# ScalarE scales the neighbouring tokens, VectorE joins them in one operation, and the key norms lie with tokens on partitions

## What is computed

```python
z = h @ w_in[l]
u_a, g_a = z[..., :D_POOL], z[..., D_POOL:2 * D_POOL]
sh = z[..., 2 * D_POOL:2 * D_POOL + D_SHIFT]          # 13 tiles of 128 channels
sh_prev = jnp.pad(sh, ((0, 0), (1, 0), (0, 0)))[:, :-1]
sh = sh + shift_mu[l] * (sh_prev - sh)                # the token shift
...
kk = heads(k * k_k)                                   # 8 heads of 64 channels
kk = kk / jnp.maximum(jnp.sqrt(jnp.sum(kk * kk, axis=-1, keepdims=True)), 1e-12)
k = k * (1.0 + (a - 1.0) * k_a)
```

## Time and profile before

| | |
|---|---|
| median of 3 runs | 1616.11 us (1614.89 to 1616.32) |
| profiled execution | 1613.78 us, its span 1612.0 us |
| TensorE busy in the span | 1548.9 us (96%) |
| VectorE, ScalarE, GpSimd busy | 788.5 (49%), 619.6 (38%), 525.0 us (33%) |
| the stage of the change | 1267 to 1408.6 us |
| VectorE busy, 1270 to 1310 us | 39.4 of 40 us |
| TensorE busy, 1300 to 1310 us | 3.2 of 10 us |
| GpSimd's weight subtraction L469 | 2425 ns in the mean |

### The profile page before, as it was taken

The page is one execution under the profiler, slowest core; times in us unless marked ns, Lnnn a source line. Parts: engine busy times, 40 slices in busy tenths (PEclk is TensorE's granted clock), DMA queues, the critical chain, the costliest instruction groups (busy, mean ns, idle before and its releaser), DMA issues.

```text
span 1612.0 us, 31406 instructions
## 1 busy us (share of the span) xinstructions
PE 1548.9 (96%) x12704; PEld 1381.6 (86%) x12704; DVE 788.5 (49%) x1374; ACT 619.6 (38%) x1139; POOL 525.0 (33%) x233
## 2 busy tenths in 40 slices
PE   8999998999999999999999999999999989999996
PEld 7898887999999999999989888888889867777765
DVE  5444443754132231575446642322316898656656
ACT  5666664443232231442224532322224534433322
POOL 2222222044444444124440444444441244450010
PEclk9999999999999999999999999999999999999998
DMA  5111111222222222223222222232222222200001
GB/s 200 53 54 53 56 64 52 67 93 92 93 94 92 93 93 92 76 80 105 91 91 80 91 93 92 93 103 92 91 92 79 66 92 78 92 16 3 3 27 52
DMA packets 35691, 125.69 MB, mean 78 GB/s; under 512 B 4080, under 2 KB 4336, under 8 KB 35568
## 3 DMA queue, kind: packets, MB, share of 16 engines
q1 hardware_dynamic: 35568, 123.90, 23.8%
HBM read 121.79 MB, written 2.10 MB: 77 GB/s over the span
## 4 chain that ended last, share of the span: by engine, by line
PE 71%; DVE 10%; issue 2%; ACT 2%; POOL 0%; DMA 0%; DVEq 0%; POOLq 0%; ACTq 0%; SPq 0%
PE G L1493 59%; PE G L1823 3%; PE ST L1823 3%; PE PO L1823 2%; PE PV L1823 2%; DVE wlo L931 1%; DVE t L1233 1%; DVE m L951 1%; PE ST L1459 1%; PE ST L1493 1%; DVE hres L958 1%; DVE acc L1383 0%; DVE z L1236 0%; POOL wlo L469 0%; DVE rstd L892 0%
## 5 line engine op out<-in xcount | busy, mean ns | idle before, releaser
L469 POOL TENSOR_TENSOR wlo<-raw,whi 128x1024 fp32r<-128x1024 f32 x207 | 501.7, 2425 | 1050.5 <-ACT whi L521 738.6
L1493 PE MATMUL G<-xh,whi 128*128 128x258 f32 (+3 forms) x1504 | 367.1, 307 | 9.4 <-DVE wlo L931 4.1
L1493 PE MATMUL G<-xl,whi 128*128 128x258 f32 (+3 forms) x1504 | 357.5, 300 | 0.0
L1493 PE MATMUL G<-xh,wlo 128*128 128x258 f32 (+3 forms) x1504 | 355.9, 299 | 1.1 <-DVE xl L899 1.1
L1493 PE MATMUL G<-ah,whi 128*128 128x256 f32 (+2 forms) x1024 | 278.3, 313 | 1.9 <-DVE al L1118 1.6
L1493 PE MATMUL G<-ah,wlo 128*128 128x256 f32 (+2 forms) x1024 | 276.6, 311 | 0.0
L1493 PE MATMUL G<-al,whi 128*128 128x256 f32 (+2 forms) x1024 | 276.5, 311 | 0.0
L1493 PEld LDWEIGHTS G<-xh,whi 128*128 128x128 f32 x1504 | 242.6, 189 | 32.9 <-issue 10.8
L1493 PEld LDWEIGHTS G<-xh,wlo 128*128 128x128 f32 x1504 | 243.9, 189 | 10.8 <-DVE xl L899 1.3
L1493 PEld LDWEIGHTS G<-xl,whi 128*128 128x128 f32 x1504 | 243.0, 189 | 9.8
L531 ACT ACTIVATE whi<-raw 128x1024 fp32r<-128x1024 f32 x96 | 101.9, 1061 | 388.3 <-PE G L1493 388.3
(11 more groups left out here) (332 smaller groups left out, 1988.1 us busy)
## 6 DMA issues: line engine op xcount, KB each, us to landing
raw<-weights_dram SPq DMA_DIRECT2D x225, 512.0 KB, 3.5
hres<-xT_dram SPq DMA_DIRECT2D x8, 264.0 KB, 4.7
out_dram<-hres SPq DMA_DIRECT2D x8, 256.0 KB, 2.1
con<-consts_dram SPq DMA_DIRECT2D x1, 512.0 KB, 7.2
mat<-mats_dram SPq DMA_DIRECT2D x1, 512.0 KB, 8.0
con<-consts_dram SPq DMA_DIRECT2D x1, 264.0 KB, 6.4
vec<-vecs_dram SPq DMA_DIRECT2D x1, 171.0 KB, 6.1
con<-consts_dram SPq DMA_DIRECT2D x1, 128.0 KB, 4.0
```

The lines of the kernel that those rows point to most:

```text
L469: nc.gpsimd.tensor_tensor(wlo[:, s], raw[:, s % 2], whi[:, s].bitcast(F32), ALU.subtract)\
L1493: last_of[0] = nc.tensor.matmul(to[:, p0:p1], wt[:, w, ws], xt[:, k, t0 - off:t1_ - off], start=k == 0 and q == 0, stop=k == KT - 1 and q ...
```

## The change

Token shift: instead of the difference and the product on VectorE, ScalarE multiplies the neighbouring tokens with mu into `t1`, and VectorE joins tile x (1 - mu) + `t1` in one operation; 1 - mu is made once for all 13 tiles (`keep`, 128x13) behind the zeroing of the pads. ScalarE's scaling of tile i stands in its loop at j = i + 1, ahead of the weight split of that step, and ahead of the whole loop ScalarE waits for `pads_set`.

Key norms: `blk` becomes the moving operand with two of its columns, and the squares the stationary one, four times 128 tokens. The result is 128x8: tokens on partitions, and for each of four token groups the two heads of the pair. Root, maximum and reciprocal work on 128x8 (`kin`). To bring the result back to channels on partitions, TensorE multiplies for each token group and head a column of `kin`, repeated 64 times as weights, with the identity: eight products of 128 moving columns onto 64 output rows in bank 6, from which L1276 (now L1282) reads. For pair 0 this stands behind block 6, for the others behind the block of step i = 3. The sum of the next pair waits until bank 6 has been read (`kk_ready`) where it waited for the root (`kn_ready`).

```diff
--- before.py
+++ after.py
@@ -218,6 +218,8 @@
         BK = sb("BK", [P, PAIRS, NCH, 2, CH], F32, second)
         bonus = sb("bonus", [P, PAIRS, SEQ], F32, second)
         g_end = sb("g_end", [P, PAIRS, NCH], F32, second)
+        keep = sb("keep", [P, 13], F32, second)
+        kin = sb("kin", [P, 8], F32, second)
         Sg = sb("Sg", [P, CH], F32, second)
         ET, B8 = (b.rearrange("p (c t) -> p c t", t=CH) for b in (k2[:], z[:, 0, 1:]))
         second.close()
@@ -781,7 +783,15 @@
             mlp(1, OUT, 3, (2, 0))
 
 
+            act.wait_ge(S("pads_set"), 4)
             for j in range(25):
+                if 1 <= j <= 13:
+                    i = j - 1
+                    act.wait_ge(tile_out, B_IN2 + j)
+                    if i >= 2:
+                        act.wait_ge(S("shifted"), i - 1)
+                    nc.scalar.activation(t1[:, i % 2, PAD:], z[:, Z_SLOT[i], 0:SEQ], ACT.Copy, scale=col(V_MU, Z_SLOT[i]))\
+                        .then_inc(S("shift_step"), 1)
                 split(B_IN2 + j + HELD, (B_IN2 + j) % 4)
                 p, i = feature_step(j)
                 if j == 1:
@@ -800,7 +810,7 @@
                 if i == 1:
 
                     act.wait_ge(S("knorm_sum"), p + 1)
-                    nc.scalar.activation(kn[:], bank(6), ACT.Sqrt).then_inc(S("kn_ready"), 1)
+                    nc.scalar.activation(kin[:], bank(6)[:, 0:8], ACT.Sqrt).then_inc(S("kn_ready"), 1)
                     act.wait_ge(S("cp_ready"), p + 1)
                     nc.scalar.activation(Gt[:], cs[:], ACT.Exp, scale=-DECAY).then_inc(S("Gt_ready"), 1)
                     nc.scalar.activation(Gi[:], cs[:], ACT.Exp, scale=DECAY).then_inc(S("Gi_ready"), 1)
@@ -1208,7 +1218,8 @@
             nc.vector.memset(z[:, :, 0:1], 0.0).then_inc(S("pads_set"), 1)
             nc.vector.memset(zu[:, :, 0:PAD], 0.0).then_inc(S("pads_set"), 1)
             nc.vector.memset(t1[:, :, 0:PAD], 0.0).then_inc(S("pads_set"), 1)
-            dve.wait_ge(S("pads_set"), 3)
+            nc.vector.tensor_scalar(keep[:], vec[:, V_MU:V_MU + 13], -1.0, 1.0, ALU.mult, ALU.add).then_inc(S("pads_set"), 1)
+            dve.wait_ge(S("pads_set"), 4)
             def input_tile(j):
 
                 b = B_IN2 + j
@@ -1227,14 +1238,9 @@
 
                     i = j - 1
                     zi = z[:, Z_SLOT[i]]
-                    dve.wait_ge(tile_out, b)
-                    if i >= 2:
-                        dve.wait_ge(S("shifted"), i - 1)
-                    nc.vector.tensor_tensor(t1[:, i % 2, PAD:], zi[:, 0:SEQ], zi[:, 1:], ALU.subtract)\
-                        .then_inc(S("shift_step"), 1)
                     dve.wait_ge(S("shift_step"), i + 1)
-                    nc.vector.scalar_tensor_tensor(zi[:, 1:], t1[:, i % 2, PAD:], col(V_MU, Z_SLOT[i]), zi[:, 1:], ALU.mult,
-                                                   ALU.add).then_inc(S("shifted"), 1)
+                    nc.vector.scalar_tensor_tensor(zi[:, 1:], zi[:, 1:], keep[:, Z_SLOT[i]:Z_SLOT[i] + 1], t1[:, i % 2, PAD:],
+                                                   ALU.mult, ALU.add).then_inc(S("shifted"), 1)
                 p, i = feature_step(j)
                 if i == 0 and p or j == 2 + 5 * PAIRS:
 
@@ -1262,9 +1268,9 @@
                 elif i == 2:
 
                     dve.wait_ge(S("kn_ready"), p + 1)
-                    nc.vector.tensor_scalar(kn[:], kn[:], 1e-12, None, ALU.max).then_inc(S("km_ready"), 1)
+                    nc.vector.tensor_scalar(kin[:], kin[:], 1e-12, None, ALU.max).then_inc(S("km_ready"), 1)
                     dve.wait_ge(S("km_ready"), p + 1)
-                    nc.vector.reciprocal(kn[:], kn[:]).then_inc(S("kr_ready"), 1)
+                    nc.vector.reciprocal(kin[:], kin[:]).then_inc(S("kr_ready"), 1)
                 elif i == 3:
 
                     dve.wait_ge(S("Gp_ready"), p + 1)
@@ -1272,8 +1278,8 @@
                     dve.wait_ge(S("shifted"), 3 * p + 3)
                     nc.vector.scalar_tensor_tensor(sg[:], zr, col(V_RK, p), k2[:], ALU.mult, ALU.mult)\
                         .then_inc(S("rk_ready"), 1)
-                    dve.wait_ge(S("kr_ready"), p + 1)
-                    nc.vector.scalar_tensor_tensor(cs[:], zk, col(V_KK, p), kn[:], ALU.mult, ALU.mult)\
+                    dve.wait_ge(S("kn_spread"), p + 1)
+                    nc.vector.scalar_tensor_tensor(cs[:], zk, col(V_KK, p), bank(6), ALU.mult, ALU.mult)\
                         .then_inc(S("kk_ready"), 1)
                     nc.vector.tensor_tensor(zr, zr, Gt[:], ALU.mult).then_inc(S("R_ready"), 1)
                     dve.wait_ge(S("kk_ready"), p + 1)
@@ -1832,6 +1838,13 @@
                     some(bank(ahead % 4), ahead % 4, range(KT), x2h, x2l, META, [(*OUT, 0, SEQ)])
                     last_of[0].then_inc(block_done, 1)
                 p, i = feature_step(j)
+                if j == 6 or i == 3 and p:
+                    pe.wait_ge(S("kr_ready"), p + 1)
+                    for t in range(4):
+                        for x in range(2):
+                            last = mm(bank(6)[ROW[x], P * t:P * t + P],
+                                      kin[:, 2 * t + x:2 * t + x + 1].to_broadcast([P, HD]), ident)
+                    last.then_inc(S("kn_spread"), 1)
                 if i == 0 and p or j == 2 + 5 * PAIRS:
                     q = (j - 2) // 5 - 1
                     pe.wait_ge(S("rk_ready"), q + 1)
@@ -1850,8 +1863,10 @@
                 elif i == 1:
                     pe.wait_ge(S("ksq_ready"), p + 1)
                     if p:
-                        pe.wait_ge(S("kn_ready"), p)
-                    mm(bank(6), blk, kn[:]).then_inc(S("knorm_sum"), 1)
+                        pe.wait_ge(S("kk_ready"), p)
+                    for t in range(4):
+                        last = mm(bank(6)[:, 2 * t:2 * t + 2], kn[:, P * t:P * t + P], blk[:, 0:P:HD])
+                    last.then_inc(S("knorm_sum"), 1)
 
 
             def both(out_, lhsT, rhs, g):
```

## The result

The changed kernel takes 1618.99 us (median of 12 runs) against 1614.16 for the kernel before beside it. The ratio is 1.0027, 95% interval 1.0020 to 1.0035: 4.4 us slower (the two medians lie 4.8 apart), where +4.3 was forecast. One of the twelve runs took 4917.54 us and is left out of the ratio. The forecast median of 1620.4 stood on the 1616.11 us of the first three runs of the kernel before. The profiled execution of the changed kernel took 1619.82 us (span 1618.0), the kernel before 1613.78 (1612.0).

The account below looks back on a forecast made before the run. VectorE's list bounds the stage's first half, up to 1308.6 us, and TensorE's work the rest. +2.8 - 1.3 + 3.9 - 1.1 = +4.3 us gave a median of 1620.4 us; the range starts at 1614.0 and leaves out 1625.5.

Parts of the forecast that it names:

- Late split (b): Stage start: ScalarE's first weight split 2.3 us late, TensorE's wait 0.89 to 3.2 us, half clock losing 1.7 us.
- Queue (c): Pair 0: scalings queued behind sigmoids and exponentials delay VectorE's joinings; last BK and pair 1's key-norm product 2.8 us late.
- four meetings: Before pair 0's last BK, VectorE operations held by GpSimd's subtractions: 8.7 us against 7.2 before, +1.5 us.
- Wait of pair 2: TensorE's 1.27 us wait ahead of pair 2's key-norm product goes: -1.3 us.
- Spreads (d): Eight TensorE products per pair spreading the norms: 1.3 us each, three behind 1308.6 us, +3.9 us.
- Narrow norms (e): TensorE's key-norm sums with two moving columns: 0.65 us for 0.86, together -1.1 us over pairs 1 to 3.
- short start: Stage start: late split costs no clock, or one GpSimd meeting falls away: 1616.3 to 1618.8 us; chance 0.24.
- Relief: First half: scalings in time, meetings unchanged, VectorE's saving takes effect: -6.6 us, 1609.5 us; chance 0.14.
- serial spreads: TensorE's column halves don't overlap, 0.9 us more per spread: +7.0, 1623.1 us; chance 0.15, shared with a meeting more.

Follow-up runs that it names:

- short_low_after: Changed kernel with GpSimd's low part of weight blocks 8 to 11 cut to 8 of 1024 columns; ratio 0.9983 to the kernel before.
- shift_only: Kernel before with the changed token shift alone, key norms as before; ratio 0.9997 to the kernel before.
- norm_only: Kernel before with the changed key norms alone, token shift as before; ratio 0.9994 to the kernel before.
- pair0_norm: Kernel before with narrow key norms for pair 0 only, token shift as before; ratio 0.9978 to the kernel before.
- pair0_all: Changed kernel with 1 - mu early, pads awaited at first scaling, scalings 2 and 3 moved ahead, narrow norms for pair 0 only; ratio 0.9986 to kernel before.
- queue_even: Changed kernel with 1 - mu early, pads awaited at first scaling, scalings 2 and 3 moved ahead, `keep` in 256 bytes; ratio 1.0005 to kernel before.
- pads_late: Changed kernel with ScalarE's wait for `pads_set` moved behind the first weight split; ratio 1.0009 to the kernel before.
- spread_twice: Changed kernel with each spread's eight products issued twice; ratio 1.0040 to the kernel before.
- pair0_even: pair0_all with `keep` in a buffer of 256 bytes; 1610.88 us, ratio 0.9976 to the kernel before.

## Why the prediction was right, and where not

End came 5.1 us late in the traces where the sum said 4.3. The mechanism came as forecast in four of five terms; the fifth, the narrow norms, was mis-sized, and one cost was not in the sum. Term by term, from t0:

**Late split (b): right.** Split behind 2.13 us of waiting (2.3 said), TensorE's wait 3.09 us (3.2 said), and the clock fell: 0.73 over the 6.1 us behind the wait, a loss of 0.27 x 6.1 = 1.6 us (1.7 said).

```profile
1272.40:1278.50 6.10, 6.02 (x20) 4.83 (x21) 2.04 (x2) 3.87 (x5) 3.85 (x3) 0.73 0.51 172
```

**Queue (c): right, 0.5 us too large.** Less the 1.02 us of chance, joining 2 ended at 1283.1 (1283.2 said), k2 was ready at 1288.3 (1288.6), joining 3 and the small norm ended at 1291.2 (1291.0), the meetings held 8.2 us (8.7), the last BK ended at 1307.6 (1308.1). X moved by 2.3 us for 2.8. The four meetings and the wait for them were the widest term, and short_low_after shows that they, not the queues alone, place X: without them it comes 4.8 us earlier.

**Wait of pair 2: right.** It went, and with it 0.27 us of latency of the product that stood behind it (1.13 us then, 0.86 without a wait): -1.5 for -1.3.

**Spreads (d): right.** 1.02 + 0.21 = 1.23 us each for 1.3; three cost 3.7 us for 3.9. Shift_only and the changed kernel, whose clock behind X is the same (low for 4.8 us), differ by 3.8 us in end - X: three spreads and the narrow norms together.

**Narrow norms (e): mis-sized.** The step that failed is 8 x 0.07 us, the pitch of one pair of records with 16 moving. They take 0.79 us and 0.13 in the block behind (11.12 for 10.99): 0.92 for 0.86, nothing saved. -1.1 was said, +0.2 came for three; the one at half clock took 1.87 for 2.08, which is counted with the clock below. The rule of the Trainium skill ("TensorE: Matmul & The Clock Gate", LDWEIGHTS), 107 ns for 128 columns of weights and so 0.85 us for eight loads, agrees with these rows within 0.1 us.

**A term that the sum had not: the clock behind X.** The stretch at the lower level (1.2 GHz) is as long in both kernels, and part of it falls in the wait, where it costs nothing. Windows of the kernel before and, below, of the changed one (us, busy times, TensorE's clock third from the end):

```profile
1308.60:1314.70 6.10, 6.10 (x17) 4.27 (x18) 5.89 (x7) 4.70 (x6) 2.57 (x1) 0.70 0.21 60
```

```profile
1308.00:1311.80 3.80, 0.00 (x0) 0.00 (x0) 3.16 (x5) 3.10 (x5) 0.00 (x0) 0.74 0.41 138
1311.90:1318.00 6.10, 6.09 (x21) 5.24 (x22) 5.33 (x5) 5.12 (x7) 2.98 (x1) 0.61 0.06 12
```

Half clock for a share s of a window gives 1 - s/2. Before: 3.1 us inside the wait and 3.7 behind it, 6.8 us in all; now 2.0 and 4.8, the same 6.8. The loss is half of what lies behind the wait: 1.8 us, now 2.4. In norm_only, with a wait of 3.27 us, all of it lies behind the wait, which ended at 1306.59:

```profile
1300.00:1310.00 10.00, 6.73 (x27) 5.53 (x26) 9.87 (x14) 6.58 (x8) 2.51 (x2) 0.83 0.18 61
1310.00:1320.00 10.00, 10.00 (x38) 8.03 (x38) 6.63 (x7) 3.00 (x5) 2.43 (x2) 0.83 0.17 54
```

That is 0.17 x 2 x 20 = 6.8 us again, and a loss of 3.4. So a wait that is cut short without going away can give back less than it seems to: 2.1 us less waiting cost 0.6 of clock here, 3.5 us less cost 1.6 in norm_only. It need not: in pair0_norm, with nearly the same wait (3.29 us), the stretch is half as long and loses 1.7 (0.09 x 2 x 20 = 3.6 us by this window, 3.4 by narrower ones):

```profile
1300.00:1320.00 20.00, 16.71 (x65) 12.79 (x64) 18.13 (x21) 10.00 (x12) 5.77 (x3) 0.91 0.20 69
```

Of the thirteen kernels that wait ahead of X, eleven have 6.8 us at the lower level there and two (pair0_norm, pair0_all) 3.4. What decides is open, and one trace of each kernel is all there is.

Together: 2.3 - 1.5 + 3.7 + 0.2 + 0.6 = 5.3, measured 5.1. The ratio said 4.4, the medians 4.8; the difference is less than that between the tail's levels. That the forecast of 4.3 fell so near owes something to luck: norms and clock cost 1.9 us more than was said, the other terms 0.9 less. Two bounds of the prediction are off by tenths in their own sums: the top of short start is 1620.4 - 1.7 = 1618.7 (1618.8 stands there), and the low end of the range comes out near 1616.3 - 2.4 - 0.3 = 1613.6 (1614.0). Neither changes what was forecast.

**The rivals.** Relief needed the scalings to be there in time. With both waits mended (queue_even) X came 2.0 us ahead of the kernel before, under a third of the 6.8 that relief was to give: VectorE still stood idle 5.6 us for scalings, and was held 8.2 us in the last stretch.

```profile
1275.62 0.91 DVE L1248 SCALAR_TENSOR_TENSOR z<-z,keep,t 128x512 f32<-128x512 f32 x1 [1.91 <-ACT t L790]
1277.55 2.44 DVE L1248 SCALAR_TENSOR_TENSOR z<-z,keep,t 128x512 f32<-128x512 f32 x1 [1.01 <-ACT t L790]
...
1290.16 2.45 DVE L1248 SCALAR_TENSOR_TENSOR z<-z,keep,t 128x512 f32<-128x512 f32 x1 [2.72 <-ACT t L790]
```

The holding is also why the halves don't add up: shift_only and norm_only are 1.6 and 1.1 us late at end, 2.7 together, the whole 5.1. The 2.4 us between lie all in X (+2.6 and -2.7 apart, +2.3 together); end - X adds up (-0.9 and +3.8 apart, +2.8 together). With the shift made, the short reciprocal takes 3.4 us off VectorE and X sees 0.3 of it, since 3.7 us of holding come back (8.2 for 4.5): about one meeting more, and a little on each. By the ratios the gap between the halves and the whole is wider (-0.5 and -1.0 us apart, +4.4 together), since the tails of both halves are shorter; whether that belongs to these kernels or to their executions is open. Short start is excluded by the 0.73 clock and by the four meetings that all took place, serial spreads by 0.88 us for 16 records.

## What to carry to other kernels

Before work is moved from the engine that sets the pace to another, look at what stands ahead of it in that engine's queue, and what the work that goes had hidden: here 7.1 us taken off VectorE turned into 8.8 us of waiting for ScalarE and longer holding by GpSimd. Apply such an edit only where the engine it relieves is the bound: narrow norms for pair 0 alone gained 3.5 us, for all four pairs nothing that could be told, since the three others cost a full TensorE 1.23 us each. And a new small buffer is better placed behind the large ones: ahead of them it moved them by 64 bytes, at some 1 us of this stage; a move by 256 bytes cost nothing here.

## What the runs showed of the hardware

**64 bytes of address.** Products of 128x128 weights with 512 moving columns took 0.2289 us each (21.97 for 96) and 0.2323 (22.30) with their moving operand 64 bytes further (the weights stayed where they were); 256 bytes further they took 0.2290 again. The products of 256 columns with the same inputs (x2h, x2l), ahead of the stage, start 118.8 ns apart in the four kernels moved by 64 bytes and 117.8 in the ten others (median over twelve in a row): 0.9%, where the 512 columns show 1.5 to 1.9. With other inputs, moved by as much, products of 256 and 258 columns show no such difference (mean of G<-xh,whi 306 ns moved, 307 not; G<-ah,whi 312 and 313).

**Who meets GpSimd.** Operations with hardly any data are held by its subtraction too: the 128x13 `keep` took 1.55 us, the 128x8 copy 2.38, where 0.14 and 0.16 are usual. The evacuations, which read PSUM and `rstd`, and the reciprocals were not held in any of these traces (no evacuation of the stage over 0.70 us, every reciprocal of 128x512 at 3.35 to 3.36).

**The clock falls in one execution and not in another at the same place.** With 12 us windows from the first chunk product on, the changed kernel has two stretches of 3.4 us at half clock in the chunk stage (0.14 x 2 x 12); norm_only ran the same work at full clock:

```profile
1474.76:1486.76 12.00, 10.08 (x278) 9.47 (x274) 11.18 (x22) 4.07 (x8) 0.00 (x0) 0.86 0.01 3
1510.76:1522.76 12.00, 11.29 (x318) 10.81 (x320) 10.27 (x23) 4.65 (x8) 0.00 (x0) 0.86 0.01 3
```

```profile
1470.40:1482.40 12.00, 9.02 (x287) 8.57 (x289) 11.28 (x23) 4.76 (x8) 0.00 (x0) 1.00 0.01 3
1506.40:1518.40 12.00, 10.66 (x340) 10.04 (x338) 10.34 (x24) 5.32 (x9) 0.00 (x0) 1.00 0.02 4
```

The kernel before has its two elsewhere, one of them behind the wait of 1.99 us; the changed kernel and norm_only have the same wait and keep the clock. Among the ten kernels not moved by 64 bytes, the four with two such stretches (before, after, pair0_norm, queue_even) have tails of 203.2 to 203.7 us, the six with one or none (shift_only, norm_only, pads_late, spread_twice, pair0_even, short_low_after) 201.6 to 202.1. It also differs between executions of one kernel: of 32 runs of the kernel before on one chip, the eight with a mean granted clock of 0.994 took 1612.4 to 1612.9 us, the fourteen with 0.991 took 1614.7 to 1616.5. The prediction took 1.99 us to be a wait that brings the clock down; it is one that can. The waits of 3.0 to 3.1 us ahead of block 4 were followed by 3.4 us at half clock in all four kernels that had them, the 1.72 us of pads_late was not. What decides is open.
